# Sixteen gate projections of a mixer in three fp32r passes, their weights split by ScalarE and VectorE

## What is computed

```python
h = _rmsnorm(x, norm_mix[l]) * (1 + sc_m) + sh_m
proj = h @ w_in[l]
qa, ka, va, cq, ckv, kr, z, xbc, dt_raw, gates = jnp.split(proj, _IN_OFFSETS, axis=-1)
...                       # two attentions give ya and yb, a state-space scan gives ys
ga, gb, gc = jnp.split(jax.nn.sigmoid(gates), 3, axis=-1)
merged = ga * (ya @ w_branch_a[l]) + gb * (yb @ w_branch_b[l]) + gc * (ys @ w_branch_c[l])
x = x + g_m * (merged @ w_out[l])
```

## Time and profile before

| | |
|---|---|
| median of 3 runs | 2475.43 us (2474.23 to 2477.43) |
| the profiled execution | 2476.12 us, its span 2474.3 us |
| TensorE matmuls busy | 2326.3 us, 94% |
| weight loads busy (overlap the matmuls) | 1986.3 us, 80% |
| VectorE, ScalarE, GpSimd busy | 1537.8, 1057.5, 59.4 us |
| second half of the mixer, first layer | starts at 329.5 us, its last product follows 100 us later |

### The profile page before, as it was taken

How to read it: one execution, slowest core, us unless ns; L and a number is a source line. 1 busy time by engine, 2 the same in 40 slices (tenths; PEclk the granted TensorE clock), 3 DMA queues, 4 the chain that set the end, 5 groups by cost and what they waited for, 6 DMA issues and landing times. The chain is left out here.

```text
span 2474.3 us, 36955 instructions
## 1 busy us (share of the span) xinstructions
PE 2326.3 (94%) x13974; PEld 1986.3 (80%) x13974; DVE 1537.8 (62%) x2867; ACT 1057.5 (43%) x1874; POOL 59.4 (2%) x73
## 2 busy tenths in 40 slices
PE   6989998999999999889999999989999999989998
PEld 3656777989976677778999899857998899857997
DVE  4787606676743563266766766684766666684665
ACT  2322333555533334354555545334554555334544
POOL 0000001200000000021000000000000000000000
PEclk8989999999999999999999999989999999989999
DMA  8745322445445522224554445313554455213542
GB/s 313 268 183 192 110 102 77 154 157 198 180 153 214 213 109 103 95 85 180 185 188 187 171 180 191 113 52 120 199 190 153 153 186 194 104 52 128 204 178 93
DMA packets 37541, 390.18 MB, mean 158 GB/s; under 512 B 4416, under 2 KB 5056, under 8 KB 5952
## 3 DMA queue, kind: packets, MB, share of 16 engines
q1 hardware_dynamic: 37440, 388.87, 42.5%
HBM read 387.80 MB, written 1.05 MB: 157 GB/s over the span
## 5 line engine op out<-in xcount | busy, mean ns | idle before, releaser
L1278 PE MATMUL bank<-h,ring 128*128 128x256 f32 x2048 | 477.3, 389 | 9.7 <-ACT h L1069 8.1
L1278 PEld LDWEIGHTS bank<-h,ring 128*128 128x128 f32 x2048 | 388.5, 193 | 101.1 <-issue 29.2
L707 DVE TENSOR_TENSOR ffn_w_lo<-ring,ffn_w_hi 128x2048 fp32r<-128x2048 f32 x126 | 288.8, 2292 | 164.8 <-ACT ffn_w_hi L656 164.7
L577 PE MATMUL bank<-ffn_hh,ffn_w_hi 128*128 128x512 f32 x1408 | 363.5, 400 | 13.3 <-DVE ffn_hh L837 11.0
L577 PEld LDWEIGHTS bank<-ffn_hh,ffn_w_hi 128*128 128x128 f32 x1408 | 258.3, 192 | 66.3 <-issue 9.0
L629 PE MATMUL bank<-ffn_g_hi,ffn_w_hi 128*128 128x256 f32 x1056 | 299.3, 283 | 6.1 <-DVE ffn_g_lo L752 6.1
L629 PE MATMUL bank<-ffn_g_lo,ffn_w_hi 128*128 128x256 f32 x1056 | 298.8, 283 | 0.0
L629 PE MATMUL bank<-ffn_g_hi,ffn_w_lo 128*128 128x256 f32 x1056 | 298.8, 283 | 0.0
L656 ACT ACTIVATE ffn_w_hi<-ring 128x2048 fp32r<-128x2048 f32 x126 | 239.8, 1903 | 0.8
L629 PEld LDWEIGHTS bank<-ffn_g_hi,ffn_w_hi 128*128 128x128 f32 x1056 | 202.7, 192 | 7.4 <-issue 7.4
L629 PEld LDWEIGHTS bank<-ffn_g_lo,ffn_w_hi 128*128 128x128 f32 x1056 | 202.7, 192 | 0.0
(11 more groups left out here) (277 smaller groups left out, 3243.2 us busy)
## 6 DMA issues: line engine op xcount, KB each, us to landing
ring<-w_in SPq DMA_DIRECT2D x244, 1536.0 KB, 6.3
x<-x_in SPq DMA_DIRECT2D x1, 1024.0 KB, 15.3
mem<-mem_in SPq DMA_DIRECT2D x1, 1024.0 KB, 4.8
y_out<-x SPq DMA_DIRECT2D x4, 256.0 KB, 2.6
con<-con_in SPq DMA_DIRECT2D x1, 801.0 KB, 6.9
par<-par_in SPq DMA_DIRECT2D x2, 302.0 KB, 15.7
work<-pos_in SPq DMA_DIRECT2D x2, 128.0 KB, 6.2
par<-par_in SPq DMA_DIRECT2D x2, 76.0 KB, 4.6
```

The costliest lines, as they stand in the source:

```text
L577: pe.matmul(up_out(j, half, False), w_hi[:, j % 2, c0:c0 + P], hh[:, k, :, :], start=k == 0, stop=False)
L707: dve.tensor_tensor(w_lo[:, j % 2, UP], ring[:, (base + j) % RING, UP], w_hi[:, j % 2, UP], ALU.subtract).then_inc(S(tag + "_up_lo"), 1)
L1278: m = pe.matmul(ps[0:m_rows, 0:T], tile(t0 + k, base)[:, 0:m_rows], rhs, start=k == 0, stop=k == len(src) - 1 and kind != "uk")
```

## The change

The sixteen gate blocks of each layer's second half join the split products. ScalarE makes their `w_high` (16 roundings of 128x1024 per layer), VectorE their low part, and TensorE runs 24 fp32r products per block in place of 8 float32 ones. The operand `h` is split once per layer in a new step `hsplit`, which stands in unit 16 of the attention: ScalarE waits until gate block 7 is done, then writes the high part into `merged_high`; VectorE writes the low part over `h` itself (`h_low` shares its memory). `first` is a step with no work; it only marks the place where the first two weight splits stand.

```diff
+AT1[16] = AT1[16] + [("hsplit", "", 0)]
-STEPS1B = ([("silu", "", 0)] + GATES[0][:1] + [("silu", "", 1)] + GATES[0][1:] + [("silu", "", 2), ("dt", "", 0)]
+STEPS1B = ([("first", "", 0), ("silu", "", 0)] + GATES[0][:1] + [("silu", "", 1)] + GATES[0][1:] + [("silu", "", 2), ("dt", "", 0)]
...
-        if s[0] == "branch":
+        if s[0] in ("branch", "proj"):
...
-    early = {0: ("y", "", 3), 1: ("y", "", 4)}
+    early = {0: ("first", "", 0), 1: ("first", "", 0)}
...
-        h = sb("h", [P, KD, T])
+        with nc.sbuf_tensor("h", [P, KD, T], F32) as h:
+            pass
+        h_low = sb("h_low", [P, KD, T], F32R)
...
-            by_pool = lambda n: units[n][0][0] == "gate"
+            by_pool = lambda n: False
...
+                                         "gate": lambda: (merged_high, h_low),
...
+                    elif step == "hsplit":
+                        act.wait_ge(S("tiles_used"), USED1["gate", 7][0])
+                        for k in range(KD):
+                            act.activation(merged_high[:, k, :], h[:, k, :], ACT.Copy).then_inc(S("h_high"), 1)
...
+                    elif step == "hsplit":
+                        for k in range(KD):
+                            dve.wait_ge(S("h_high"), k + 1)
+                            dve.tensor_tensor(h_low[:, k, :], h[:, k, :], merged_high[:, k, :],
+                                              ALU.subtract).then_inc(S("h_low"), 1)
```

## The result

| | median, us | runs | ratio to before, 95% interval |
|---|---|---|---|
| before (same chip) | 2475.65 (2471.12 to 2480.71) | 9 | |
| changed | 2482.24 (2479.31 to 2490.35) | 9 | 1.0029 [1.0015, 1.0042] |

The changed kernel is 6.6 us slower. Its profiled execution took 2485.52 us, its span is 2483.7.

The account below looks back on a forecast made before the run. TensorE is 94% busy, but in the changed stretches waits for ScalarE and VectorE at each seam. +4.6 us first layer and +1.3 second sum to +5.9: 2476.12 to 2482.0 profiled, median 2481.3; range 2473 to 2489.

Parts of the forecast that it names:

- step 7: Both layers, behind the second `xt` wait: TensorE's clock falls once, +1.7 us on the path; falls in the scan cost nothing.
- 1. `hsplit`: Before the barrier after gate block 7: eight ScalarE copies of `h` shift the barrier by 3.0 us (up to 3.8).
- 2. The four roundings: From the barrier to the first `xt` copy: four ScalarE roundings add 2.6 us; second `xt` shifts 5.6, waiting near 7 us.
- 3. U3 and U4: Gate blocks behind the second `xt`: each 0.65 us shorter, but ScalarE's roundings delay the `xt` copies; net +0.45 us.
- the 2.1 given as the sign: Expected waits of 2.1 us before the fourth `xt` and before the transposes of `dt`.
- 4. U5 to U8: Gate blocks U5 to U8: weights ready in time, each block 0.65 us shorter, together -2.6 us.
- step 5: Fourth `cb`: waits for VectorE's multiplication of the third, behind a late remainder; +1.6 us, and U9's gain is hidden.
- 6. The scan on VectorE: First `y` to eighth `decay`: VectorE becomes the bound, 41.0 us for 43.2 before, a gain of 2.2 us.
- more falls: Rival: longer waits before U0, U5, U9 bring more clock falls; two more in each layer give 2488 us; chance 0.2.

Follow-up runs that it names:

- e1: Changed kernel with GpSimd instead of ScalarE rounding the weights of the first four gate blocks of each second half: 2486.06 us, ratio 1.0039.
- e3: Changed kernel with the weight split of U10 moved from behind U8 to behind the fourth `cb`: 2490.43 us, ratio 1.0058.
- e2: Changed kernel with twelve extra float32 products, their result unread, placed ahead of the second `xt`: 2484.83 us, ratio 1.004.
- e5: Changed kernel with the high part of `h` made earlier, without waiting for gate block 7: 2481.57 us, ratio 1.0026.
- e4: Changed kernel without VectorE's weight remainders for U11 to U15, the third pass reading rounded weights instead: 2482.77 us, ratio 1.003.
- e6: Changed kernel with all sixteen gate roundings of a layer on GpSimd: 2483.48 us, ratio 1.0034.
- e8: Changed kernel with third `silu` and `dt` moved behind first `xt` copies, `h` rounded early, all sixteen roundings on GpSimd: 2475.22 us, ratio 1.0002.

## Why it came out so, step by step

Shifts of the changed kernel against before, each counted from the start of gate block 7 (324.27 and 976.17 before, 324.12 and 983.68 after), in us. The forecast's column is made of the prediction's terms, with the fall of the clock of step 7.

| start of | first layer | forecast | second layer | forecast |
|---|---|---|---|---|
| second `xt` | +5.72 | +5.6 | +6.79 | +5.6 |
| U5 | +7.77 | +7.8 | +7.78 | +6.1 |
| last `cb` | +8.43 | +6.8 | +6.94 | +5.1 |
| first `y` | +9.42 | +6.8 | +6.83 | +5.1 |
| second pair of `brA` | +8.17 | +4.6 | +3.72 | +1.3 |

1. `hsplit`, right: ScalarE's first instruction behind the barrier moves from 329.47 to 332.44, 3.1 us counted from gate block 7, for +3.0.
2. The four roundings, right in the first layer, to 0.1 us (a full-clock block takes 2.84 us, U1, for 2.85): the second `xt` at 349.77 for 349.8. The wait is 5.70 and not 7, because U0 starts at 333.59 and runs at half clock at first (1.84 us to its second pass), so TensorE is through U2 1.5 us later than I had it. In the second layer the half clock lasts all three passes and comes through: ScalarE has to wait 1.30 us for U0's end, and the `xt` is 1.2 us later than forecast.
3. U3 and U4, right in the first layer: +2.05 with the clock, for 0.45 + 1.7. In the second it is +0.99 for 0.45, since the fall at U3 lasts longer than before. The waits are 1.47 and 1.56 us; the 2.1 given as the sign was a slip, for by the step's own terms the 0.78 before `dt`'s transposes grows by 0.87, to 1.65.
4. U5 to U8 and 5, the fourth `cb`: in the second layer -0.84 from U5 to the last `cb`, for -1.0 by both terms, and in the first a fall of the clock at U5 takes 1.5 us back. The fourth `cb` waits for VectorE's L1673, as step 5 said.
6. The scan on VectorE: from the first `y` to the end of the eighth `decay` 42.0 us (390.04 to 432.02), for 41.0 forecast and 43.2 before. Three of the waits for ScalarE's exponential are 1.0 us and not 0.7, and one remainder waits 0.79 us for its `w_high`. The mechanism holds, and the gain, 1.2 us, is a little over half of the 2.2 forecast. In the second the scan is 3.1 us shorter, for 3.8. Part of both gains is clock: the kernel before has a fall at U10 in each layer (8.86 and 9.20 us for two blocks that take 7.14 at full clock), the changed kernel none behind the first `y`.
7. The clock is the step that was too small. It counted one fall in each layer, 1.7 us, and said that falls in the scan cost nothing. There are falls at U0 and U3 in both layers, two more in the first, at U5 and at the fourth `cb`, and one more in the second, at U9. The one at the fourth `cb` costs TensorE 3.2 us, of which 1.0 reaches the first `y`; that at U9 costs 1.7 and is hidden, since the `y` waits for VectorE there. The granted clock at U9 of the second layer:

```profile
1042.70:1047.30 4.60, 4.60 (x26) 4.43 (x25) 3.44 (x7) 2.08 (x4) 0.00 (x0) 0.63 0.13 56
```

This is the rival "more falls", by part of its size. That falls in the scan cost nothing is true of short ones only (e1, e3).

So the stages of the profiled execution give +11.9 for +5.9. The medians give +6.6 for +5.9, and part of this closeness is luck: the rest of the program, which the change does not touch, is 2.5 us shorter in the changed kernel's trace, and this execution is 3.3 us above its own median. Over all the kernels measured the rest of the program takes 2259 to 2269 us; what sets that is not known.

## What to carry to other kernels

Before a busy engine's work is made shorter by work on others, ask in the changed stretch, not over the whole span, what each wait ends on. Here TensorE was 94% busy, but at every seam it waited for ScalarE or VectorE, and those two got the new work, so 0.65 us saved per block turned into longer waits and those waits into half clock. The same reading named the cheap edit: what stood ahead of ScalarE's copy had no need to, and moving two of its steps back, the third `silu` and `dt`, brought 11 us (7 by the order, the rest by a clock that stayed up), where 32 cheaper blocks cost 7.

## What the runs showed of the hardware

- TensorE's clock. In the changed kernel it fell behind each wait of 5.7 us and also at U0, which has waits of 3.02 and 1.86 us with a few small products ahead of it. It once kept its clock behind a wait of 3.65 us, and once did not the earlier trace rows. Behind the same wait of 1.56 us U5 lost its clock in the changed kernel's first layer and kept it in the second; in e1, e2 and e5 it was the other way round, and in e4 it was kept twice. A fall cost TensorE 1.4 us (U0, first layer) to 3.2 us (fourth `cb` to the end of U9), and what it did to the path went from nothing (U9, second layer) to all of it (U3). So falls can't be costed one by one.
- GpSimd rounds 128x1024 to fp32r in 1.04 us, as fast as ScalarE (1.05). Beside VectorE instructions that read two SBUF operands the two delay each other. Of the four VectorE instructions at 390.77 in e6, this view of their line in that window gives the shortest, the median and the longest in ns, and the timeline shows that the longest is the first:

```profile
390.77 1.22 DVE L1695 SCALAR_TENSOR_TENSOR work<-work 128x128 f32<-128x128 f32 x1 [0.70 <-ACT work L1539]
...
L1695 DVE SCALAR_TENSOR_TENSOR work<-work x4: 337/338/1224, 390.8 to 392.4; 128x128 f32<-128x128 f32 x4
```

It took 0.89 us longer than the others and ended at 391.99, just behind GpSimd's rounding (390.81 to 391.85). The Trainium skill (SBUF — State Buffer, SBUF: two separate sides) says that the two engines' shared ports are locked for a whole instruction by whichever starts first, while the other blocks fully. The trace agrees that one goes through at its full speed while the other waits, in both directions: the roundings that start inside a VectorE instruction took 1.58 us in e6 and 2.76 in e8. It does not bear out that the first to start wins each time, for at 390.77 VectorE's start is recorded 0.04 us before GpSimd's.
